# Seven products in place of eight from pair 3 on, not pair 4, in two feed-forward stages

## The chip, the cores and the metric

The kernel runs on one core of a Trainium2 chip. The time is device time of the whole program in microseconds (us), median of several runs. PE is TensorE, DVE is VectorE, ACT is ScalarE, POOL is GpSimd, SP is the engine that issues most of the weight transfers.

## What is computed

The program is two transformer-like blocks on one sequence of 512 tokens and width 1024; the second block also has 256 context tokens. All of it is float32. What the change touches is the second block's gated feed-forward, which is applied to the 512 tokens twice: first with `ffn_w_in[0]` (here the x stage), and again at the end with `ffn_w_in[1]` (the y stage).

```python
D_MODEL, D_FF, SEQ, CTX_LEN = 1024, 2816, 512, 256

def swiglu(y, w_in, w_out):
    a, b = jnp.split(y @ w_in, 2, axis=-1)
    return (jax.nn.silu(a) * b) @ w_out

# in second_block, for its one layer:
x  = ada_out(x,  swiglu(ada_in(x,  mod,  0, norm_pre[l, 0]), ffn_w_in[l, 0], ffn_w_out[l, 0]), ...)   # x stage
xc = ada_out(xc, swiglu(ada_in(xc, modc, 0, norm_pre[l, 0]), ffn_w_in[l, 0], ffn_w_out[l, 0]), ...)   # context
...                                                                                                  # token mixing
x  = ada_out(x,  swiglu(ada_in(x,  mod,  2, norm_pre[l, 2]), ffn_w_in[l, 1], ffn_w_out[l, 1]), ...)   # y stage
```

## The kernel before

**Layout.** Features lie on the 128 partitions, tokens along the free dimension. Each float32 operand is split in a high and a low part (HH and HL for the normed tokens, WH and WL for weights, GH and GL for hidden values), and every product is made of three matmuls: high by high, high by low, low by high (`mm3`, lines 643 to 646). ACT makes the high part of a weight chunk by a copy, DVE makes the low part by a subtraction. A chunk is 128 x 1024 floats (512 KB), lands in one of 4 places of `stage`, and its two parts go to one of 3 places of WH and WL.

**A stage.** The 22 output tiles of `a` and the 22 of `b` are taken in two halves of 11 pairs (tile j and tile 22 + j). After each half, 8 tiles of the down projection add up its 11 hidden tiles. In half 0 the first `FAST_FROM[0]` = 4 pairs, jj = 0 to 3, are made by eight: each of the two tiles is 8 blocks of k times 3 matmuls of 512 columns, so a pair is 48 matmuls of 512 columns and two chunks. The other pairs, and all of half 1, are made by seven (`fast_pairs`): the pair of tiles, cut in two halves of tokens and two halves of k, is a 2 x 2 block product made from 7 products (A11, A12, A22 by the weights themselves, S1 to S4 by sums and differences of weights) of 4 blocks times 3 matmuls of 256 columns. A pair by seven is 84 matmuls of 256 columns and the same two chunks.

**What the seven products need.** DVE makes four weight sums per pair (`weight_sum_of`, line 3417, 128x512 each) and the low part of seven operands (`low_unit`, line 3423); ACT makes seven high parts (`high_unit`, 2276) and copies the running sum out three times (`keep`, 2297); DVE joins the blocks (3452 to 3468). Once per stage, the tokens need sums too: POOL restores the normed tokens as HH + HL into Z (`restored`, 4140, four instructions, which start when the last low part of the norm is made); DVE makes four differences from it (`token_differences`, 3425 to 3432, which begins with a wait for the last of POOL's four); ACT and DVE split the results (`high_sum`, `low_sum`).

**The order around the change.** Every engine runs a list written out by hand. In half 0 of a stage of 512 tokens DVE does, for each jj (lines 3507 to 3529):

```python
if n == S and jj == FAST_FROM[0] - 2:
    token_differences(who)
step("sb" if pair else "sa", who, half, jj)
if jj and n == S:
    hidden_low(jj - 1)
if n == S and jj == FAST_FROM[0] - 1:
    for q in (3, 2, 4):
        low_sum(who, q)
    for q in (1, 3, 2, 4):
        weight_sum_of(r, 0, q)
if not pair:
    step("sb", who, half, jj)
...
made(e.tensor_tensor(T, bank("sb", who, half, jj)[:, 0:n], T, ALU.mult), "sb", who, half, jj)
```

The last line (3527) is the gate product of pair jj; it waits for PE to end the pair's second tile. `step` splits chunks up to two beyond the one named, and passes over the chunks of pairs by seven. Between the second `step` and the last line, at jj = `FAST_FROM[0] - 1`, stand the low parts of the first four operands (`low_unit`). ACT's list has the same shape: at jj = `FAST_FROM[0] - 1` it makes the high parts of three token sums (2344) between the hidden values of the pair before and the gate of this one, then the first four operands' high parts, the last token sum, the hidden values of this pair, and the next two operands (2352 to 2361).

**The y stage has fewer pairs by eight left.** The tile a of pair 0, the tile b of pair 0 and the tile a of pair 1 are made by PE beside the norm, block by block (`firsts`), so that after the norm PE begins with tile b of pair 1 (lines 1319 to 1325). In the x stage all of pair 0 is made with the last steps of the norm, and PE has pairs 0 to 3 ahead of it.

**Other things set by the number of pairs.** `pair_number` counts the pairs by seven of a stage through both halves, and its parity says where weight sums and kept blocks lie (CB or X in the x stage, CB or MST in the y stage). A pair by eight takes two PSUM banks of a ring of six and two ticks of `walk`, a pair by seven three banks and none. The ticks set at which of the context's tiles the steps of the next norm are slipped in (three ticks of four, line 217).

Of the kernel before, what the change touches and what calls it, by code (L numbers as in the profile page):

```python
# [21 lines left out]
POOL_PARTS = (((0, 0), (0, 1), (0, 2), (0, 3), (1, 0)), ((1, 1), (1, 2), (1, 3)), ((2, 0), (2, 1)), ((2, 2), (2, 3)),  # L22
              ((3, 0), (3, 1)), ((3, 2), (3, 3)))
POOL_BY_VECTOR = (0, 3, 5)
FAST_FROM = (4, 0)


def fast_order(r):

    last = 10 - FAST_FROM[r]  # L30
    order = [(0, "A11"), (0, "A12")]
# [200 lines left out]
def program(nc, ws, wm, xT, cT, params, cond, consts, max_rows, out, plan):  # L232
# [3 lines left out]
    with ctx:  # L236
# [207 lines left out]
        def place_products(r, first):  # L444
# [6 lines left out]
            ring_place["next"] = v + (len(FAST[r]) - 1) // 2  # L451
            for n in range(11 - FAST_FROM[r % 2]):
                for part in range(2):
# [13 lines left out]
        def pair_number(r, n):  # L467
            return r % 2 * (11 - FAST_FROM[0]) + n

        def two_before(r, n):  # L470

            g, first = pair_number(r, n) - 2, r - r % 2
            if g < 0:
                return None
            return (first, g) if g < 11 - FAST_FROM[0] else (first + 1, g - 11 + FAST_FROM[0])

# [142 lines left out]
        def tensor(e):  # L619
# [655 lines left out]
            def fast_pairs(r):  # L1275
# [4 lines left out]
                upto["fast", r] = first  # L1280
                for n in range(11 - FAST_FROM[r % 2]):
                    j = 11 * (r % 2) + FAST_FROM[r % 2] + n
                    for c in (j, 22 + j):
# [3239 lines left out]
```

## Time and profile before

| | |
|---|---|
| time, median of 3 runs | 2908.78 us (2908.39 to 2909.41) |
| the profiled execution: its time | 2908.46 us |
| the profiled execution: its span, first to last instruction | 2906.6 us |
| PE busy | 2895.6 us, 16089 matmuls |
| DVE busy | 2009.2 us, 3123 instructions |
| ACT busy | 1249.1 us, 2027 instructions |
| POOL busy | 262.2 us, 210 instructions |
| DMA | 393.39 MB, mean 135 GB/s |

PE is busy in all of the span's 40 slices and the granted clock is full in all of them. A busy PE is not PE at its peak, as matmuls overlap and their ends are modelled; what counts is the time from the start of one matmul to the start of the next.

### The profile page before, as it was taken

Reading aid. Unit: us, or ns where it says so; the run is one execution under the profiler, and the core shown is the slowest. Engines: PE = TensorE matmul, PEld = TensorE weight load, DVE = VectorE, ACT = ScalarE, POOL = GpSimd, SP = SyncE. Lnnn points to the kernel's source line nnn. Section 1 sums busy time; section 2 is a strip of 40 time slices with the busy share of each in tenths; the row PEclk is TensorE's granted clock in tenths of the full one; section 3 lists DMA queues with packets and bytes.
Section 4 is the critical chain, followed back from the end, with each engine's and each line's share of the span. In section 5 each row is a group of like instructions: output and inputs, shape, how many; then the busy total and the mean of one; then the engine's idle time right before and its main releaser. Section 6 shows DMA issues by size and latency. Waiting matters only on the chain. (4 is left out here: it accounts for less than half of the span.)

```text
span 2906.6 us, 40025 instructions
## 1 busy us (share of the span) xinstructions
PE 2895.6 (100%) x16089; PEld 2523.6 (87%) x16089; DVE 2009.2 (69%) x3123; ACT 1249.1 (43%) x2027; POOL 262.2 (9%) x210
## 2 busy tenths in 40 slices
PE   9999999999999999999999999999999999999999
PEld 8988888888888888888888889899989887899997
DVE  7867666865768776767866746775847667486684
ACT  4433333432534333423433435454635457455462
POOL 0300000000001200100000002100003006210001
PEclk9999999999999999999999999999999999999999
DMA  8454446344443433343443445432345331213222
GB/s 309 158 170 152 158 159 202 124 145 138 145 145 109 152 123 108 122 138 127 162 139 135 147 147 180 138 108 89 110 160 182 125 120 62 73 66 111 100 98 78
DMA packets 113962, 393.39 MB, mean 135 GB/s; under 512 B 12649, under 2 KB 16233, under 8 KB 113777
## 3 DMA queue, kind: packets, MB, share of 16 engines
q1 hardware_dynamic: 89136, 303.70, 31.0%
q10 hardware_dynamic: 24640, 87.12, 9.2%
q8 instruction: 128, 2.10, 0.3%
q14 instruction: 58, 0.47, 0.1%
HBM read 384.47 MB, written 6.31 MB: 134 GB/s over the span
## 5 line engine op out<-in xcount | busy, mean ns | idle before, releaser
L644 PE MATMUL ps<-HH,WH 128*128 128x512 f32 (+1 forms) x2152 | 778.5, 362 | 0.1
L645 PE MATMUL ps<-HL,WH 128*128 128x512 f32 (+1 forms) x2152 | 775.0, 360 | 0.0
L646 PE MATMUL ps<-HH,WL 128*128 128x512 f32 (+1 forms) x2152 | 774.7, 360 | 0.0
L2804 DVE TENSOR_TENSOR WL<-stage,WH 128x1024 fp32r<-128x1024 f32 x424 | 530.1, 1252 | 341.8 <-ACT WH L1860 341.2
L644 PE MATMUL ps<-GH,WH 128*128 128x256 f32 (+2 forms) x2110 | 696.8, 330 | 1.2 <-ACT X L2297 0.5
L645 PE MATMUL ps<-GL,WH 128*128 128x256 f32 (+2 forms) x2110 | 694.8, 329 | 0.0
L646 PE MATMUL ps<-GH,WL 128*128 128x256 f32 (+2 forms) x2110 | 694.7, 329 | 0.0
L1860 ACT ACTIVATE WH<-stage 128x1024 fp32r<-128x1024 f32 x427 | 448.1, 1052 | 280.1 <-PE ps L646 271.7
L646 PEld LDWEIGHTS ps<-HH,WL 128*128 128x128 f32 x2152 | 406.5, 189 | 61.6
L644 PEld LDWEIGHTS ps<-HH,WH 128*128 128x128 f32 x2152 | 406.7, 189 | 59.6 <-issue 1.1
L645 PEld LDWEIGHTS ps<-HL,WH 128*128 128x128 f32 x2152 | 406.7, 189 | 58.0
L644 PEld LDWEIGHTS ps<-GH,WH 128*128 128x128 f32 x2110 | 400.6, 190 | 39.9 <-DVE WL L3423 1.1
L645 PEld LDWEIGHTS ps<-GL,WH 128*128 128x128 f32 x2110 | 400.8, 190 | 37.4
L646 PEld LDWEIGHTS ps<-GH,WL 128*128 128x128 f32 x2110 | 400.7, 190 | 36.1
L1880 ACT ACTIVATE GH<-SCR 128x512 fp32r<-128x512 f32 (+5 forms) x310 | 166.2, 549 | 414.6 <-DVE SCR L3142 125.3
L2831 DVE CUSTOM_DVE_ANT_0 MST<-MST,CB,PAR 128x1024 f32<-128x1024 f32 x158 | 206.1, 1305 | 1.8 <-DMA MST<-wm 1.3
L2846 DVE TENSOR_TENSOR GL<-SCR,GH 128x512 fp32r<-128x512 f32 (+1 forms) x192 | 124.5, 657 | 63.1 <-ACT GH L1880 61.4
L4038 POOL TENSOR_TENSOR GL<-SCR,GH 128x512 fp32r<-128x512 f32 (+3 forms) x102 | 121.5, 1210 | 411.4 <-ACT GH L1880 410.8
L2178 ACT ACTIVATE SCR<-ps,PAR 128x512 f32<-128x512 f32 x88 | 68.2, 777 | 153.2 <-PE ps L646 138.3
L4016 POOL TENSOR_TENSOR V<-V,HM 128x4 f32<-128x4 f32 (+1 forms) x20 | 25.7, 1284 | 977.7 <-DVE V L2874 637.0
L3274 DVE SCALAR_TENSOR_TENSOR SCR<-ps,PAR,SCR 128x511 f32<-128x511 f32 x88 | 65.8, 748 | 62.3 <-ACT SCR L2178 62.3
L2276 ACT ACTIVATE WH<-stage 128x512 fp32r<-128x512 f32 x108 | 67.5, 630 | 58.1 <-PE ps L646 58.1
(378 smaller groups left out, 3432.2 us busy)
## 6 DMA issues: line engine op xcount, KB each, us to landing
stage<-ws SPq DMA_DIRECT2D x533, 512.0 KB, 3.4
MST<-wm ACTq DMA_DIRECT2D x154, 512.0 KB, 3.4
Z<-wm SPq DMA_DIRECT2D x10, 512.0 KB, 9.3
TAB<-consts ACTq DMA_DIRECT2D x7, 448.0 KB, 3.8
MST<-wm SPq DMA_DIRECT2D x6, 512.0 KB, 8.8
away<-X SPq DMA_DIRECT2D x8, 256.0 KB, 4.5
X<-away SPq DMA_DIRECT2D x8, 256.0 KB, 3.9
Z<-max_rows ACTq DMA_DIRECT2D x8, 256.0 KB, 4.5
```

Of the source, the lines that this page charges most:

```text
L644: e.matmul(o, wh, mh, start=start, stop=False, **more)
L645: e.matmul(o, wh, ml, start=False, stop=False, **more)
L646: return e.matmul(o, wl, mh, start=False, stop=stop, **more)
L1860: e.activation(wh, src, ACT.Copy).then_inc(whi.sem, whi.up(("w", i)))
L1880: e.activation(dst, src, ACT.Identity if "bias" in more else ACT.Copy, **more).then_inc(hi.sem, hi.up(name))
L2178: e.activation(T, bank("up", l, c)[:, :], ACT.Identity, scale=par("cw", (l * 3 + 1) * 44 + c), bias=par("cb", l * 44 + c)).then_inc(ev.sem ...
L2276: e.activation(unit(r, n, p)[0], unit_source(r, n, p), ACT.Copy).then_inc(whi.sem, whi.up(("u", r, n, p)))
L2804: e.tensor_tensor(wl, src, wh.bitcast(F32), ALU.subtract).then_inc(wlo.sem, wlo.up(("w", i)))
L2831: e.tensor_tensor_reduce(out=products, in0=a, in1=b, scale=1.0, scalar=res if i else bias, op0=ALU.mult, op1=ALU.add, accum_out=res).then_inc(
L2846: e.tensor_tensor(dst, src, high_part.bitcast(F32), ALU.subtract).then_inc(lo.sem, lo.up(name))
L3274: made(e.scalar_tensor_tensor(out=T[:, 1:S], in0=p[:, 0:S - 1], scalar=par("cw", (l * 3) * 44 + c), in1=T[:, 1:S], op0=ALU.mult, op1=ALU.a ...
L4038: e.tensor_tensor(dst, src, high_part.bitcast(F32), ALU.subtract).then_inc(plo.sem, plo.up(name))
```

## The change

One constant: the first pair by seven in half 0 is pair 3, not pair 4. In each of the two stages, pair 3 is made by seven products in place of eight, half 0 has 8 pairs by seven in place of 7, and everything that was written relative to `FAST_FROM[0]` is one pair earlier: the token differences on DVE stand at the head of pair 1 and not of pair 2, and the split token sums, the first weight sums and the first four operands stand in pair 2 and not in pair 3.

```diff
-FAST_FROM = (4, 0)
+FAST_FROM = (3, 0)
```

The order of the products within half 0 follows from it: `fast_order(0)` lists 56 products in place of 49. The number of chunks stays the same; `pair_number` in half 1 grows by one, so that its parity changes; the bank ring is one place further on after each stage, and `walk` has counted two ticks fewer when the second context half begins.

## Rows read from the trace of the kernel before

**Rows 1.** The page, part 1: busy us (share of the span) x instructions.

```profile
PE 2895.6 (100%) x16089; PEld 2523.6 (87%) x16089; DVE 2009.2 (69%) x3123; ACT 1249.1 (43%) x2027; POOL 262.2 (9%) x210
```

**Rows 2.** Stretches: bounds and length, busy us (x) of PE, PEld, DVE, ACT, POOL, clock, DMA.

```profile
1825.43:1868.98 43.55, 43.55 (x195) 36.05 (x193) 28.48 (x28) 15.41 (x21) 12.21 (x4) 1.00 0.44 134
1888.86:1898.94 10.08, 10.08 (x86) 10.08 (x85) 9.34 (x18) 6.32 (x12) 0.00 (x0) 1.00 0.34 112
...
2564.19:2591.42 27.23, 27.23 (x123) 22.54 (x121) 21.88 (x24) 13.48 (x18) 6.40 (x3) 1.00 0.19 60
```

**Rows 3.** Timeline of PE, y stage: start, us, instruction, count, idle before and releaser.

```profile
2564.19 0.40 PE L644 MATMUL ps<-HH,WH 128*128 128x512 f32 x1
...
2575.10 0.39 PE L644 MATMUL ps<-HH,WH 128*128 128x512 f32 x1
...
2580.54 0.39 PE L644 MATMUL ps<-HH,WH 128*128 128x512 f32 x1
...
2591.42 0.28 PE L644 MATMUL ps<-HH,WH 128*128 128x256 f32 x1
...
2594.65 0.36 PE L644 MATMUL ps<-GH,WH 128*128 128x256 f32 x1 [0.20 <-DVE GL L2846]
...
2608.08 0.35 PE L644 MATMUL ps<-GH,WH 128*128 128x256 f32 x1 [0.26 <-ACT TAB L2297]
```

**Rows 4.** Timeline of DVE, y stage.

```profile
2567.58 0.75 DVE L2846 TENSOR_TENSOR GL<-SCR,GH 128x512 fp32r<-128x512 f32 x1 [0.70 <-ACT GH L1880]
2569.02 2.65 DVE L2804 TENSOR_TENSOR WL<-stage,WH 128x1024 fp32r<-128x1024 f32 x1 [0.69 <-ACT WH L1860]
2571.59 0.68 DVE L3527 TENSOR_TENSOR SCR<-ps,SCR 128x512 f32<-128x512 f32 x1
2572.20 1.21 DVE L3427 TENSOR_TENSOR TAB<-Z 128x1024 f32<-128x1024 f32 x1
...
2576.85 1.22 DVE L2804 TENSOR_TENSOR WL<-stage,WH 128x1024 fp32r<-128x1024 f32 x1
2577.99 0.68 DVE L2846 TENSOR_TENSOR GL<-SCR,GH 128x512 fp32r<-128x512 f32 x1
...
2580.74 0.69 DVE L3527 TENSOR_TENSOR SCR<-ps,SCR 128x512 f32<-128x512 f32 x1 [0.93 <-PE ps L646]
...
2589.03 1.29 DVE L3423 TENSOR_TENSOR WL<-stage,WH 128x512 fp32r<-128x512 f32 x2
...
2591.62 0.69 DVE L3527 TENSOR_TENSOR SCR<-ps,SCR 128x512 f32<-128x512 f32 x1
2592.71 1.22 DVE L2846 TENSOR_TENSOR HL<-TAB,HH 128x1024 fp32r<-128x1024 f32 x1 [0.40 <-ACT HH L1880]
```

**Rows 5.** Timeline of POOL, the restored tokens of the x and the y stage.

```profile
1825.29 12.36 POOL L4140 TENSOR_TENSOR Z<-HH,HL 128x1024 f32<-128x1024 f32 x4 [29.63 <-DVE HL L2850]
...
2559.76 10.84 POOL L4140 TENSOR_TENSOR Z<-HH,HL 128x1024 f32<-128x1024 f32 x4 [7.76 <-DVE HL L2850]
```

**Rows 6.** Line 4140: count, shortest, median and longest in ns, first and last start.

```profile
L4140 POOL TENSOR_TENSOR Z<-HH,HL x8: 2394/3084/3388, 1825.3 to 2567.7; 128x1024 f32<-128x1024 f32 x8
```

**Rows 7.** Timeline of ACT, y stage.

```profile
2592.59 0.61 ACT L1880 ACTIVATE GH<-SCR 128x512 fp32r<-128x512 f32 x1
...
2594.15 0.36 ACT L2297 ACTIVATE TAB<-ps 128x256 f32<-128x256 f32 x1
```

**Rows 8.** Timeline of DVE, x stage.

```profile
1837.07 0.69 DVE L3527 TENSOR_TENSOR SCR<-ps,SCR 128x512 f32<-128x512 f32 x1 [1.69 <-ACT SCR L2349]
1837.95 1.23 DVE L2804 TENSOR_TENSOR WL<-stage,WH 128x1024 fp32r<-128x1024 f32 x1 [0.18 <-ACT WH L1860]
...
1847.42 0.69 DVE L3527 TENSOR_TENSOR SCR<-ps,SCR 128x512 f32<-128x512 f32 x1 [2.58 <-PE ps L646]
```

**Rows 9.** Timeline of POOL, second context half, the norm's root.

```profile
2223.49 1.93 POOL L4016 TENSOR_TENSOR V<-V,HM 128x4 f32<-128x4 f32 x1 [5.13 <-DVE V L2874]
```

**Rows 10.** Timeline of PE, second context half, the spread that waits for that root.

```profile
2226.02 0.38 PE L773 MATMUL ps<-IDN,V 128*128 128x128 f32 x2
```


## Prediction

> **What bounds the kernel now.** I read the page's busy times first: PE is busy for the whole span, every other engine for 69% of it at most [rows 1]. So time goes only where matmuls start later or fewer columns are pushed. Then I read stretches of PE by windows, to get the price of a pair by either method. In the x stage the four pairs by eight fill 1825.43 to 1868.98, 43.55 us, at a granted clock of 1.00 [rows 2]; that is 10.89 us a pair. The window counts 195 matmuls, as it takes those that reach in from the neighbours; 4 times 48, or 192, start in it, one each 0.227 us. One steady pair by seven fills 1888.86 to 1898.94, 10.08 us for 84 matmuls of 0.120 us each [rows 2]. The five quarters of tile pairs of the y stage (120 matmuls) fill 27.23 us, 5.45 us a tile [rows 2]. PE has no gap in any of these. Last I read the timelines around the place where the token sums are made, as the change moves these and nothing there belongs to PE.
>
> **The saving.** Pair 3 costs 10.89 us by eight and 10.08 by seven, so 0.81 us in each of two stages, 1.6 us in all, 0.06% of the time. It is small because 84 matmuls have 12.5% fewer columns than 48 of double width, but a matmul costs some 13 ns beside its columns: 0.227 is not twice 0.120 [rows 2]. In a pair by seven DVE is busy for 9.34 of 10.08 us, ACT for 6.32, and the weight loads all of the time [rows 2]. One more such pair, in a row of them, therefore keeps PE's pace; its weight sums, operands and joins (some 30 instructions on DVE and ACT by that window, in place of 8) hide there, and DVE keeps 0.74 us to spare. Where that cover failed, in the first pairs of a row, PE stood 0.2 to 0.3 us at a time [rows 3]; that price is taken up below.
>
> **What is moved.** The token differences go from the head of pair 2 to the head of pair 1 in DVE's list, and they wait for POOL's four restoring sums, which cannot start before the norm's last low part. Behind that wait in DVE's queue stand the hidden low part of pair 0, the low part of the chunk of tile b of pair 2, and the gate product of pair 1; behind the last of these wait ACT's hidden values and three token sums, DVE's token sums, weight sums and first operands, and so PE's first product by seven.
>
> **The x stage.** POOL's four sums run 1825.29 to 1837.65 [rows 5]. DVE ends the gate product of pair 0 at 1837.76 [rows 8], where the differences will now stand: no wait. They take 4.65 us (2572.20 to 2576.85 in the y stage, where they follow one another [rows 4]), to 1842.4. The chunk that DVE split at 1837.95 [rows 8] then ends at 1843.6, and PE wants it, for tile a of pair 2, at 1825.43 + 2 x 10.89 = 1847.2. That leaves 3.6 us. The gate product of pair 1 still starts at 1847.42, waiting for PE [rows 8]. The first operand's low part is ready 9.0 us after the start of the gate product that heads this chain (2580.74 to 2589.03, and the first 0.7 of that row [rows 4]), so at 1856.4; PE wants it at 1858.1. Cost nothing, gain 0.81.
>
> **The y stage.** Here PE is three tiles further on, and the same chain is late.
> First, the end of POOL. Its four sums run 2559.76 to 2570.60 [rows 5]. At their shortest they take 2.394 us each [rows 6], 9.6 in all, so 2569.3 at the earliest; 2570.6 is the other end. I take 2570.1, since the last of them overlapped the hidden low part of 2567.58 [rows 4], which now comes later. That DVE and POOL hold each other up shows in DVE's split of 2569.02: 2.65 us where the same instruction takes 1.22 at 2576.85, and it ends 1.1 us after POOL does [rows 4, 5]. The Trainium skill, page "SBUF — State Buffer", section on the shared port pair, calls this an exclusive lock held for a whole instruction; by that rule 2570.1 is right, and by POOL's time as it stands it would be 2570.6 and the sum 0.5 more.
> Second, DVE: differences to 2574.8 (4.65), hidden low part to 2575.4 (0.6, the step from 2577.99 to the next), the chunk of tile b of pair 2 to 2576.7 (1.22). PE wants that chunk at 2575.10 [rows 3]: a first wait of 1.6 us. In the kernel before it had been split from 2569.02 to 2571.67 [rows 4].
> Third, the gate product of pair 1 starts at 2576.6, and with it the chain that before started at 2580.74 [rows 4]; the first operand is ready 9.0 us later, 2585.6. PE has ended tile b of pair 2 at 2576.7 + 5.45 = 2582.2. A second wait of 3.4 us.
> Fourth, what follows. The third product waits for the running sum's copy, which ACT makes after the hidden values of the last pair by eight (2592.59, copy 2594.15 [rows 7], product 2594.65 [rows 3]), and a product of the second pair waited until 2608.08 [rows 3], again for a chain that runs through DVE's list. That list stood 0.5 us for PE in between (0.1 before 2591.62, 0.4 at 2592.71 [rows 4]), and will not now; I take 0.6 us as regained, 0 to 0.8 as bounds. Before, 2608.08 is 27.3 us after 2580.74. After, it is 26.7 us after 2576.6, so 2603.3, and one more pair by seven follows: 10.08.
> So the y stage ends 2603.3 + 10.1 - 2608.1 = 5.3 us later. With POOL at 2569.3 and 0.8 regained it is 4.3; with POOL at 2570.6 and nothing regained, 6.4.
>
> **The sum.** Minus 0.81 in the x stage, plus 5.3 in the y stage: 4.5 us on the profiled execution's own 2908.46 us, 2912.9 or 2913.0. The median of the runs is 0.3 above that execution, so 2913.2, with 2912.2 to 2914.4 by the bounds. That is 0.15% slower; about 0.2%, 5.8 us, is what a measurement of this kernel can tell from no change, so the verdict would be the same time.
>
> **Small edits.** The bank ring is one place further in the token mixing between the stages; every bank there is freed by an evacuation that other instructions of the same stretch wait for anyway: nothing, within 0.5 us either way. `walk` starts the second context half two ticks earlier in its count of four, so that a norm's first sums and its spread, which stood two ticks apart, are neighbours. The other norm of that half shows what neighbours do: its root ends at 2225.42 [rows 9] and PE takes the spread at 2226.02 without idling [rows 10]. It is 0.6 us short of costing; I take nothing, up to 1 us.
>
> **Rivals.**
> *The waits are hidden.* If DVE's list held the chunk of tile b of pair 2 in time and the chain behind it ran faster, only the saving is left: 2907.2. For that the differences would have to start by 2568.6 (2575.1 less 1.22, 0.6 and 4.65), which is before POOL's sums can end even at their shortest, 2569.3. It speaks against this only that the waits are worked out from one execution. Chance 0.10; a part of the waits only, 2909 to 2912, 0.08.
> *The clock falls.* Before, the granted clock is 1.00 in these stretches and PE's longest waits in the part looked at are 0.20 and 0.26 us [rows 2, 3], so no row shows what a wait of 3.4 us does. If the clock fell to the lower of its levels, 1.2 in place of 2.4 GHz, at that wait, the two products behind it would take 5.8 us and not 2.9, and end at 2591.4; the third could start at 2590.1 otherwise (2594.65 was 13.9 us after 2580.74, less the 0.4 regained by then), so 1.3 us are lost; each further product at that level costs 1.44 more. With none to three of them, 2914.5 to 2918.8. The page "TensorE: Matmul & The Clock Gate" of the Trainium skill, Part 1, says that an idle array falls to the lower level; by that rule this is where the kernel could meet it. Chance 0.14. This is the case on the slower side; it decides if the wait before the first product by seven is as long as worked out, or longer.
> *DVE does not catch up.* With 93% of DVE taken in each pair by seven [rows 2], an instruction that comes late in pair 0 could hold PE in pairs 1 to 3 again. Each time costs 0.4 to 0.5 us, the steps from one product to the next at 2594.65 and 2608.08 beside the usual 0.12, for three to six times: 2914.5 to 2916. Chance 0.10.
>
> **How the numbers follow.** The forecast has 0.56 and 2913.2. Slower by over 0.2% (above 2914.6): the clock, the list that does not catch up, and a small end of the forecast, 0.26. Faster by over 0.2% (below 2903.0) would need a gain that no row offers, 0.02. The same: 0.72. The range takes in the hidden waits below and most of the clock's case above: 2907 to 2917.
>
> **What would show it.** Right: two gaps on PE in the y stage, some 1.6 us before tile b of pair 2 and some 3.4 us before the first product by seven, both ended by DVE; DVE idle before its first token difference until POOL ends; no gap in the x stage, where the first product by seven starts near 1858. Wrong: no gap in the y stage, a granted clock below 1.00 there, or gaps in the x stage.

## The result, and the profile after

The time after is 2912.8 us (median, 2912.25 to 2914.04), 1.0014 times the time before, with a 95% interval of 1.0008 to 1.002. That is 4.0 us, or 0.14%, slower: below the 0.2% that the forecast took as the same, though the interval reaches that bound. The interval lies above 1 throughout, so the kernel is slower by more than the noise. The forecast was 2913.2. The profiled execution's own time is 2912.28 us, its span 2910.5, against 2908.46 and 2906.6 before.

Part 1 of the page after, as in [rows 1]:

```profile
PE 2895.6 (99%) x16161; PEld 2527.3 (87%) x16161; DVE 2017.3 (69%) x3149; ACT 1255.2 (43%) x2043; POOL 261.0 (9%) x210
```

PE has 72 matmuls more, 36 in each of the two stages, and the same busy time, but it fills 99% of the span and no longer all of it. The second view of the kernel after is its stretches: bounds and length, busy us (x) of PE, PEld, DVE, ACT and POOL, granted clock, DMA share and GB/s. The first two are half 0 of the x stage, pairs by eight and then the rest to the first product of the down projection; the third is half 0 of the y stage after the norm; the last two lie inside it.

```profile
1825.32:1857.99 32.67, 32.67 (x146) 27.04 (x145) 24.66 (x24) 12.30 (x17) 12.21 (x4) 1.00 0.48 146
1857.99:1939.72 81.73, 81.09 (x674) 80.74 (x673) 72.84 (x130) 49.99 (x94) 0.00 (x0) 1.00 0.33 110
2562.92:2666.88 103.96, 99.22 (x747) 95.55 (x746) 89.41 (x149) 60.13 (x108) 5.95 (x3) 0.98 0.28 92
2584.00:2588.00 4.00, 3.57 (x20) 3.60 (x21) 4.00 (x7) 2.37 (x5) 0.00 (x0) 0.66 0.41 131
2588.00:2592.00 4.00, 4.00 (x33) 4.00 (x33) 3.97 (x7) 2.66 (x7) 0.00 (x0) 0.92 0.00 0
```

The same stretches of the kernel before, in the same columns: half 0 of the x stage in one, and half 0 of the y stage.

```profile
1825.43:1940.70 115.27, 114.54 (x782) 106.70 (x781) 91.05 (x140) 59.24 (x103) 12.21 (x4) 1.00 0.37 116
2564.19:2662.86 98.67, 98.21 (x710) 93.17 (x709) 84.46 (x136) 57.34 (x100) 6.40 (x3) 1.00 0.28 92
```

The x stage went from 115.27 to 32.67 + 81.73 = 114.40 us, a gain of 0.87. The y stage went from 98.67 to 103.96, a loss of 5.29, and PE is now busy for 4.74 us less than its stretch, where it lacked 0.46 before. The whole trace of after stands 1.27 us earlier at the y stage's start (2562.92 for 2564.19): 0.11 from before the x stage, 0.87 from the x stage, 0.2 from the second context half (below), 0.09 from the rest. To compare a time of the y stage with the forecast, 1.27 has to be added to it.

The waits of PE over the whole kernel after, by line waited for (us in total, times, longest), the first three:

```profile
PE ps L644 <- DVE WL L3423: 3.2, 1, 3.2
PE ps L644 <- POOL GL L4038: 1.8, 6, 0.7
PE ps L644 <- DVE WL L2804: 1.6, 1, 1.6
```

The first and the third are new, one time each, and both are in the y stage. PE's timeline shows them (start, us, instruction, count, idle before and what ended it):

```profile
2573.60 0.39 PE L646 MATMUL ps<-HH,WL 128*128 128x512 f32 x1
2575.55 0.47 PE L644 MATMUL ps<-HH,WH 128*128 128x512 f32 x1 [1.55 <-DVE WL L2804]
...
2580.88 0.39 PE L646 MATMUL ps<-HH,WL 128*128 128x512 f32 x1
2584.43 0.36 PE L644 MATMUL ps<-HH,WH 128*128 128x256 f32 x1 [3.16 <-DVE WL L3423]
...
2588.87 0.30 PE L644 MATMUL ps<-GH,WH 128*128 128x256 f32 x1
...
2602.01 0.36 PE L644 MATMUL ps<-GH,WH 128*128 128x256 f32 x1
```

A wait is read from start to start, less the 0.23 us at which these matmuls follow one another otherwise: 1.95 less 0.23 is 1.7 us before tile b of pair 2, and 3.55 less 0.23 is 3.3 us before the first product by seven. DVE's and POOL's timelines in the same place show why, DVE's with the rows of before in [rows 4], POOL's in [rows 5]:

```profile
2558.48 10.39 POOL L4140 TENSOR_TENSOR Z<-HH,HL 128x1024 f32<-128x1024 f32 x4 [7.76 <-DVE HL L2850]
...
2564.92 0.69 DVE L3527 TENSOR_TENSOR SCR<-ps,SCR 128x512 f32<-128x512 f32 x1 [5.38 <-ACT SCR L2349]
2568.91 1.23 DVE L3427 TENSOR_TENSOR TAB<-Z 128x1024 f32<-128x1024 f32 x1 [3.29 <-POOL Z L4140]
...
2573.58 0.68 DVE L2846 TENSOR_TENSOR GL<-SCR,GH 128x512 fp32r<-128x512 f32 x1
2574.18 1.22 DVE L2804 TENSOR_TENSOR WL<-stage,WH 128x1024 fp32r<-128x1024 f32 x1
2575.32 0.68 DVE L3527 TENSOR_TENSOR SCR<-ps,SCR 128x512 f32<-128x512 f32 x1
...
2584.80 1.29 DVE L3423 TENSOR_TENSOR WL<-CB,WH 128x512 fp32r<-128x512 f32 x2
2586.01 0.68 DVE L3527 TENSOR_TENSOR SCR<-ps,SCR 128x512 f32<-128x512 f32 x1
```

DVE ends the gate product of pair 0 (2564.92) and then stands for 3.29 us, until POOL's last restoring sum ends at 2568.87. The four differences follow, then the hidden low part, and only then the chunk (2574.18) for which PE waits at 2575.55; the gate product of pair 1, which heads the chain to the first product by seven, starts at 2575.32.

In the x stage the same list runs without such a wait: DVE's first difference follows the gate product at once, and the gate product of pair 1 still waits 2.12 us for PE. The first product by seven starts at 1857.99.

```profile
1836.96 0.69 DVE L3527 TENSOR_TENSOR SCR<-ps,SCR 128x512 f32<-128x512 f32 x1 [1.69 <-ACT SCR L2349]
1837.57 1.22 DVE L3427 TENSOR_TENSOR Z<-Z 128x1024 f32<-128x1024 f32 x1
...
1847.31 0.69 DVE L3527 TENSOR_TENSOR SCR<-ps,SCR 128x512 f32<-128x512 f32 x1 [2.12 <-PE ps L646]
```

### The profile page after: what moved, and what is told of

Read it like the earlier page. It is cut to its first block, busy times and chain, and to the rows that moved or that the text cites. A ratio compares the mean times of both kernels' runs of the same rounds, so it can differ in the third digit from the quotient of the medians.

```text
span 2910.5 us, 40223 instructions
## 1 busy us (share of the span) xinstructions
PE 2895.6 (99%) x16161; PEld 2527.3 (87%) x16161; DVE 2017.3 (69%) x3149; ACT 1255.2 (43%) x2043; POOL 261.0 (9%) x210
## 4 chain that ended last, share of the span: by engine, by line
PE 97%; DVE 1%; POOL 1%; issue 1%; ACT 1%; DMA 0%; POOLq 0%; DVEq 0%; ACTq 0%
PE ps L644 30%; PE ps L645 30%; PE ps L646 30%; PE ps L859 1%; PE ps L874 1%; PE ps L860 1%; PE ps L773 1%; PE ps L738 1%; PE ps L710 0%; PE ps L711 0%; PE ps L714 0%; POOL Z L4140 0%; POOL GL L4038 0%; PE ps L747 0%; PE ps L1522 0%
## 5 line engine op out<-in xcount | busy, mean ns | idle before, releaser
L2804 DVE TENSOR_TENSOR WL<-stage,WH 128x1024 fp32r<-128x1024 f32 x420 | 523.1, 1247 | 339.2 <-ACT WH L1860 338.7
```

The costliest lines, as they stand in the source:

```text
L2804: e.tensor_tensor(wl, src, wh.bitcast(F32), ALU.subtract).then_inc(wlo.sem, wlo.up(("w", i)))
```

## The experiments

The theory: the x stage gains about 0.8 us, and the y stage loses about 5.3, because DVE's list waits there for POOL's restored tokens and hands its lag on to PE. The rivals: first, the loss is not of one stage (the ring, the ticks, the parities); second, the y stage's loss is that of the fallen clock, of which the 0.66 above is a sign; third, DVE's list is late in the y stage for itself, whatever POOL does. Times are compared with the kernel before on the same chip: 2908.74 us for e0, e1, e2 and e6, 2908.97 for e3 to e5, and 2908.76 for e7 to e9. Medians of one kernel differ by up to 0.2 us here (2912.80 for after and 2912.59 for e0, 2907.39 for e1 and 2907.46 for e9); the intervals of the ratios are wider, about 0.0009 either way. One profiled execution differs from the next too: e0's, of the same kernel as after, has 114.24 us in half 0 of the x stage and 104.22 in that of the y stage, where after has 114.40 and 103.96.

### The changed kernel again, and each stage alone

`e0_after` is the kernel after. For `e1_x_only` and `e2_y_only` the constant gets an entry for each half of each stage, and every place that used it takes the one of its own stage:

```diff
-FAST_FROM = (3, 0)
+FAST_FROM = (3, 0, 4, 0)    # e1: x stage as changed, y stage as before
+FAST_FROM = (4, 0, 3, 0)    # e2: x stage as before, y stage as changed
```

> The changed kernel again, as the yardstick of this group: 4.0 us above the kernel before by every theory. In its trace PE should show the two gaps of the y stage (some 1.7 us before tile b of pair 2, some 3.3 us before the first product by seven).

> Pair 3 by seven in the x stage alone. Theory of DVE's list (the loss is the wait for POOL's restored tokens in the y stage, nothing else): 0.8 us below the kernel before, no gap on PE in either stage. Rival, a pair by seven costs more than it saves wherever it stands: 2 us above the kernel before, half of the loss.

> Pair 3 by seven in the y stage alone. Theory of DVE's list: all of the loss and none of the gain of the x stage, 4.8 to 5.3 us above the kernel before, with both gaps. Rival, a pair by seven costs more wherever it stands: 2 us above.

Measured: e0 2912.59 (1.0014, interval 1.0005 to 1.0023), e1 2907.39 (0.9996, 0.9987 to 1.0004), e2 2913.70 (1.0017, 1.0008 to 1.0026). Against before these are +3.85, -1.35 and +4.96 us. The two halves add up to +3.6, so the loss has its place, the y stage, and needs nothing of the x stage. PE's waits in e2 are those of after within 0.05 us:

```profile
2574.53 0.39 PE L646 MATMUL ps<-HH,WL 128*128 128x512 f32 x1
2576.44 0.47 PE L644 MATMUL ps<-HH,WH 128*128 128x512 f32 x1 [1.53 <-DVE WL L2804]
...
2581.78 0.39 PE L646 MATMUL ps<-HH,WL 128*128 128x512 f32 x1
2585.32 0.36 PE L644 MATMUL ps<-HH,WH 128*128 128x256 f32 x1 [3.16 <-DVE WL L3423]
```

The gain of e1 has the sign and about the size of the forecast, but its interval holds 1: by itself it is not told from no change. What it has beyond the 0.8 is partly the stretch from the first matmul of the x stage's second down projection (the one behind half 1, 2111.44 before) to the matmul behind the last spread of the second context half (2281.88 before), which takes 170.44 us before, 170.46 in e2, and 170.24, 170.22 and 170.23 in after, e1 and e9: 0.2 us less wherever the x stage is changed. The traces show where: before and e2 have two short waits of PE there, before the matmuls at 2204.84 and 2216.44 of the kernel before, that after, e1 and e9 lack. The first comes right behind the end, at 2204.69, of a chunk's low part that DVE made beside POOL and that took 2.31 us. That the ticks, which move the next norm's steps, are what removes these waits is argued; no run changes the ticks alone.

### POOL's end, earlier and later

`e4_half_restored` has POOL make two of its four restoring sums in the y stage, so that it ends some 4.7 us earlier; `e5_one_more_restored` gives it a fifth sum, into a place that nobody reads then, ahead of the second.

```diff
 # e4, y stage
-            for k in range(0, 8, 2):
+            for k in (0, 6):
 # e5, y stage, inside the loop over k
+                if k == 2:
+                    e.tensor_tensor(MST[:, 1, :]..., HH[:, 0:2, :]..., HL[:, 0:2, :]..., ALU.add)
```

> The changed kernel with two of POOL's four restoring sums left out in the y stage (the other tiles of Z keep old values). Theory of DVE's list: the differences start right behind the gate product of pair 0, 3.2 us earlier, the first gap goes and the gap before the first product falls to 1.8 us: 3.2 us below the changed kernel, 0.8 us above the kernel before. Rival, the clock: with no long wait it stays up, and a further 1.3 us come back, 4.5 us below the changed kernel. Rival, POOL has nothing to do with it: no change.

> The changed kernel with a fifth sum of the same size on POOL in the y stage, ahead of the second (its result is not used). Theory of DVE's list: all that follows is 2.4 us later, so 2.4 us above the changed kernel, 6.4 above the kernel before. Rival, the wait is partly hidden behind another one: less than that. Rival, the clock: more than that, as PE stands longer.

Measured: e4 2909.48 (1.0002, 0.9993 to 1.0011), +0.5 against before and 3.3 less than e0 by that; e5 2915.26 (1.0022, 1.0013 to 1.0031), +6.3 against before and 2.4 more than e0. A sum of POOL's more is a sum of PE's time more. The first fence is DVE and PE in e4, the second in e5.

```profile
2565.37 0.69 DVE L3527 TENSOR_TENSOR SCR<-ps,SCR 128x512 f32<-128x512 f32 x1 [5.39 <-ACT SCR L2349]
2565.98 1.22 DVE L3427 TENSOR_TENSOR TAB<-Z 128x1024 f32<-128x1024 f32 x1
...
2579.49 0.39 PE L646 MATMUL ps<-HH,WL 128*128 128x512 f32 x1
2581.49 0.35 PE L644 MATMUL ps<-HH,WH 128*128 128x256 f32 x1 [1.61 <-DVE WL L3423]
...
2585.87 0.36 PE L644 MATMUL ps<-GH,WH 128*128 128x256 f32 x1 [1.27 <-ACT TAB L2297]
```

```profile
2571.38 1.23 DVE L3427 TENSOR_TENSOR TAB<-Z 128x1024 f32<-128x1024 f32 x1 [5.64 <-POOL Z L4140]
...
2573.74 0.39 PE L646 MATMUL ps<-HH,WL 128*128 128x512 f32 x1
2578.02 0.50 PE L644 MATMUL ps<-HH,WH 128*128 128x512 f32 x1 [3.90 <-DVE WL L2804]
...
2586.90 0.36 PE L644 MATMUL ps<-HH,WH 128*128 128x256 f32 x1 [1.55 <-DVE WL L3423]
```

In e4 the wait for POOL is gone, the first wait of PE with it, and the second is 2.00 less 0.23, 1.8 us in place of 3.3. So POOL accounts for about 3.3 us of the y stage's loss by the medians, and for 2.9 by the stretch of its half 0 (101.04 us in e4, 103.96 in after). It doesn't account for all: with POOL out of the way DVE's differences, 4.65 us of work, still stand ahead of the chain. The kernel is no faster than before: with the 1.35 us that e1 gained, the y stage of e4 is some 1.9 us behind, and by the stretch (98.67 before) 2.4. PE waits there 1.8 us for the first operand and then twice for ACT's copy of the running sum, 1.3 us before the third product and 0.5 later. So for this remainder the third rival holds, and ACT's list has a part in it; that is read from e4's trace, and no run takes the differences themselves away. In e5 DVE idles 2.35 us more than in after, and the two waits of PE are 4.28 less 0.23, 4.1 us, and 1.95 less 0.23, 1.7 us: together 5.8 for the 5.0 of after; half 0 of the y stage takes 106.40 us there, 2.4 more than in after. That the second is shorter than in after has to do with the clock, next.

### Is it the clock?

The granted clock of after is 0.66 in the stretch behind its second wait: the lower level for part of it. `e6_busy_wait` gives PE twelve matmuls of ones to do in that wait.

```diff
                 upto["fast", r] = first
+                if r == 2:
+                    warm(12)
```

> The changed kernel with 12 matmuls of ones (512 columns, some 2.7 us, result unused) on PE in the wait before the first product by seven of the y stage, so that PE is busy there and its clock need not fall. Theory of DVE's list: the first two products run at the full rate (2.9 us and not 4.3), but the third still waits for the running sum's copy, so the time is that of the changed kernel within 0.3 us. Rival, the fallen clock is what costs: 1.3 to 1.6 us below the changed kernel.

Measured: 2912.66 (1.0013, 1.0004 to 1.0022), beside 2912.59 for e0 on the same chip. The stretch behind the wait now has its full clock, and the third product waits instead (the stretch first, then the gate product of pair 1 on DVE and PE's timeline; the edit adds two lines to the file, so that line 3527 is 3529 here):

```profile
2584.00:2588.00 4.00, 3.55 (x26) 2.97 (x25) 4.00 (x7) 2.37 (x5) 0.00 (x0) 1.00 0.36 122
```

```profile
2575.86 0.68 DVE L3529 TENSOR_TENSOR SCR<-ps,SCR 128x512 f32<-128x512 f32 x1
...
2584.89 0.39 PE L644 MATMUL ps<-HH,WH 128*128 128x256 f32 x1 [0.45 <-DVE WL L3425]
...
2587.75 0.28 PE L646 MATMUL ps<-HH,WL 128*128 128x256 f32 x1
2589.36 0.36 PE L644 MATMUL ps<-GH,WH 128*128 128x256 f32 x1 [1.33 <-ACT TAB L2299]
```

From the first product by seven to the third it is 2589.36 - 2584.89 = 4.47 us at the full clock, and 2588.87 - 2584.43 = 4.44 in after at the fallen one. Two products take 24 x 0.120 = 2.88 us at the full clock, so the lower level did cost 1.56 us in after, but of time in which PE would have waited for ACT's copy of the running sum. What times the third product is the chain from the gate product of pair 1: from the one's start to the other's it is 13.50 us in e6, 13.49 in e4 and in e5, all three at the full clock behind the second wait, and 13.55 in after, e0 and e2 (2575.32 to 2588.87 in after), all three at the fallen one. The clock fell and cost some 0.05 us. In e5 it fell behind the first wait: the granted clock of 2578 to 2582 is 0.57 there. The matmuls of tile b of pair 2 that it slowed stand ahead of a wait of DVE's making, and that wait became shorter by as much (1.7 us, not 3.3).

### The differences one place later

`e3_differences_later` puts the token differences of the y stage behind the gate product of pair 1, nearer to where they stood before.

```diff
-                    if n == S and jj == FAST_FROM[0] - 2:
+                    if who == "x" and jj == FAST_FROM[0] - 2:
                         token_differences(who)
 ...  # behind the gate product, line 3527
+                    if who == "y" and jj == FAST_FROM[0] - 2:
+                        token_differences(who)
```

> The changed kernel with the y stage's token differences moved on DVE behind the chunk of tile b of pair 2 and behind the gate product of pair 1. Theory of DVE's list: the first gap goes, the chain to the first product becomes 1.6 us shorter (hidden part and chunk no longer stand between POOL's end and the differences' end), so 1.6 us below the changed kernel; the gap before the first product by seven becomes 3.6 us. The chunk's split now meets POOL and takes 2.6 us and not 1.2. Rival, POOL's end alone sets the chain, whatever stands behind it in the list: no change.

Measured: 2911.34 (1.0008, 0.9999 to 1.0017), +2.4 against before and 1.5 less than e0 by that; 1.2 less by the two medians themselves and by the stretch of half 0 of the y stage (102.74 us, 103.96 in after). DVE no longer stands, and splits the chunk of tile b of pair 2 ahead of the differences; the first wait is gone and the second a little longer. DVE's and PE's timeline, and the stretch behind the wait:

```profile
2567.71 2.65 DVE L2804 TENSOR_TENSOR WL<-stage,WH 128x1024 fp32r<-128x1024 f32 x1 [0.69 <-ACT WH L1860]
2570.28 0.68 DVE L3527 TENSOR_TENSOR SCR<-ps,SCR 128x512 f32<-128x512 f32 x1
2570.89 1.21 DVE L3427 TENSOR_TENSOR TAB<-Z 128x1024 f32<-128x1024 f32 x1
...
2579.01 0.39 PE L646 MATMUL ps<-HH,WL 128*128 128x512 f32 x1
2582.91 0.35 PE L644 MATMUL ps<-HH,WH 128*128 128x256 f32 x1 [3.51 <-DVE WL L3423]
```

```profile
2583.00:2587.00 4.00, 3.02 (x24) 2.81 (x24) 4.00 (x7) 2.38 (x5) 0.00 (x0) 1.00 0.40 131
```

So this order of DVE's list is worth 1.2 to 1.5 us of the loss: the work of the differences has to be done before the first product by seven wherever they stand. It is the one other order that was tried, and the y stage does not gain by it.

### How much room the x stage has

The prediction put the room in the x stage at 3.6 us. `e7_x_one_more` and `e8_x_two_more` are e1 with one and with two sums more on POOL in the x stage, 2.4 us each, into a place that nobody reads then; `e9_x_only_again` is e1 once more, beside them.

```diff
 # x stage, inside the loop over k; e7 has range(1), e8 range(2)
+                if k == 2:
+                    for i in range(2):
+                        e.tensor_tensor(CB[:, i, :]..., HH[:, 0:2, :]..., HL[:, 0:2, :]..., ALU.add)
```

> Pair 3 by seven in the x stage alone, once more, as the yardstick of the two runs beside it: 1.3 us below the kernel before as measured earlier, 0.8 by the price of a pair.

> Pair 3 by seven in the x stage alone, with a fifth sum of the same size on POOL in the x stage, ahead of the second (its result is written over). Theory that the x stage has room: DVE's differences start 2.4 us later, but PE wants the next chunk 3.6 us after it was ready, so within 0.4 us of the kernel without the fifth sum. Rival, the first product hangs on POOL in the x stage too: 2.4 us more.

> The same with two such sums, 4.8 us on POOL. Theory that the x stage has room of 3.6 us: now it is used up, the gate product of pair 1 starts some 2.6 us later than PE would allow, and with it all of DVE's list; 2 to 3 us above the kernel without the extra sums, with two gaps on PE as in the y stage, a short one before tile a or b of pair 2 and one of some 1 us before the first product by seven. Rival, it hangs on POOL throughout: 4.8 us more. Rival, it never hangs on POOL: no change.

Measured: e9 2907.46 (0.9996, 0.9986 to 1.0005), e7 2907.23 (0.9996, 0.9987 to 1.0004), e8 2908.84 (1.0001, 0.9992 to 1.001). DVE's first difference in e7, then in e8 the same and PE's two waits behind it:

```profile
1842.25 1.23 DVE L3427 TENSOR_TENSOR Z<-Z 128x1024 f32<-128x1024 f32 x1 [2.25 <-POOL Z L4140]
```

```profile
1842.21 1.22 DVE L3427 TENSOR_TENSOR Z<-Z 128x1024 f32<-128x1024 f32 x1 [4.61 <-POOL Z L4140]
...
1846.84 0.39 PE L646 MATMUL ps<-HH,WL 128*128 128x512 f32 x1
1848.25 0.47 PE L644 MATMUL ps<-HH,WH 128*128 128x512 f32 x1 [1.03 <-DVE WL L2804]
...
1863.25 0.36 PE L644 MATMUL ps<-GH,WH 128*128 128x256 f32 x1 [0.96 <-ACT X L2297]
```

A wait of DVE of 2.25 us costs nothing: half 0 of the x stage takes 114.43 us in e7 and 114.52 in e9. (The profiled execution of e7, 2909.41 us, is 2 us longer than its median; its x stage begins at 1827.67 and not 1825.68, so these lie ahead of it.) A wait of 4.61 costs PE 1.41 less 0.23, 1.2 us, at the chunk that PE wants next: 4.6 less 1.2 is 3.4 us of room, near the 3.6 worked out. The time of e8 is 1.4 above e9, and its half 0 of the x stage 1.6 longer (116.13). I had expected 2 to 3, with a second wait ahead of the first product by seven. That wait did not come; a wait of 1.0 us for ACT before the third product came in its place, and behind it PE made up part of the lag.

## Why the prediction was right

**The mechanism and both terms held.** The x stage gained 0.87 for the 0.81 worked out, with the first product by seven at 1857.99 for "near 1858". The y stage lost 5.29 for 5.3. That the last digits agree is luck: e0, the same kernel, gained 1.03 in the x stage and lost 5.55 in the y stage. The y stage's steps, with 1.27 added to the times of after: POOL ended at 2570.14 (2570.1 forecast); the gate product of pair 1 started at 2576.59 (2576.6); the first product by seven at 2585.70 (2585.6); the product that stood at 2608.08 [rows 3] at 2603.28 (2603.3); the two waits of PE were 1.7 and 3.3 us (1.6 and 3.4). That POOL would end 0.5 us sooner, since the hidden low part moved out of its way, is borne out: its four sums took 10.39 us in after, and 10.84 in the kernel before [rows 5]. In e3, where the hidden low part (2566.28) and the chunk's split run beside POOL again, they take 10.84 again, all of it more in the fourth sum (2.86 us, begun at 2566.42, for 2.41 in after), and the split takes 2.65 us, as in [rows 4]. The rule of the Trainium skill, page "SBUF — State Buffer", section "SBUF: two separate sides", that one of the two holds the pair for a whole instruction, agrees with these rows.

**Where the 5.3 us lie.** From the start of the stage to the first product by seven it is 21.51 us after (2562.92 to 2584.43) and 27.23 before, with one pair by eight less: -5.72. From there to the product of the second pair in the row 17.58 after (to 2602.01) and 16.66 before [rows 3]: +0.92, as DVE's and ACT's lists still lag. One pair by seven more: +10.08. The sum is +5.28. The prediction had all three inside its third and fourth steps.

**Points that it had to choose.** The small edits came out slightly below nothing: 0.2 us were gained in the second context half, whose steps `walk` shifts, where nothing, up to a loss of 1 us, had been put. The sum of the terms, -0.87 - 0.2 + 5.29, is 4.2; the span differs by 3.9 and the medians by 4.0. The 0.2% that the prediction gave as what a measurement can tell from no change was too coarse: the interval of the result is 0.06% to either side.

**The rivals.** The waits were not hidden: DVE's differences waited for POOL in after, and even in e4, without that wait, a wait of 1.8 us was left. The clock did fall, as the second rival said it might, at the wait that it named. A granted clock below 1.00 in the y stage stood in the prediction's own list of what would show it wrong, so that sign came true while the time held. The rival's price was wrong in one place: it let the first two products run at the lower level from end to end, 5.8 us, and so pass the time at which the third could start. They took 4.44 us, since the granted clock was 1.00 over 2584 to 2585, 0.50 over 2586 to 2588 and 0.67 over 2588 to 2589, and the third, forecast to be free at 2590.1, started at 2588.87 + 1.27 = 2590.14. How long the clock would stay low was not forecast; that the fall fitted into a wait for ACT was luck. DVE did catch up: over the whole half 0 of the y stage PE shows no wait beyond the two. (That rival's 0.4 to 0.5 us a time are the whole steps; less the usual 0.12 they are 0.36 and 0.42.)

**What stays open.** Whether it is the ticks that shorten the context half by 0.2 us; how the 1.9 to 2.4 us that e4 leaves in the y stage divide between DVE's list and ACT's; and whether the y stage can gain at all with another order of DVE's and ACT's lists, which the runs only bound: with the wait for POOL taken away, e4 is still 0.5 us above before.

## What to carry to other kernels

A step that moves earlier in a list worked off in order moves its wait too: look up when its input is ready, on an engine that may be off the path, and what stands behind it in the list. One constant that serves two stages has two costs, as the same list had 3.4 us of room in one stage and stood 3.3 us for POOL in the other, where PE waited for what came behind it; here the change alone to the x stage (2907.39 and 2907.46) had a median some 1.3 us below the kernel before, though its interval does not tell it from no change. A gap of PE, or a fallen clock behind it, costs only what the next wait on PE's path does not take back.

## What the runs showed of the hardware

The lower clock showed itself as 256-column matmuls 0.21 us apart (after, 2586.24 and 2586.46) in place of 0.120. What makes it fall is not the length of the wait alone: behind a wait of 3.3 us in after the granted clock was 0.66 over the next 4 us, behind one of 4.1 us in e5 it was 0.57, and behind one of 3.7 us in e3 it stayed at 1.00. With twelve matmuls in the wait (e6) it stayed at 1.00 too. Ahead of the one in after lay 5.6 us of matmuls and another wait, of 1.7 us; ahead of those in e3 and e5 PE had no other wait in this stage. Whether that is what decides it was not tested. The Trainium skill, page "TensorE: Matmul & The Clock Gate", Part 1, has the array fall to its lower level when idle; after and e5 agree, e3 does not show it.
